# Gated DeltaNet and sparse attention block: decays formed in the place of L, its norms on VectorE, inverse blocks in one transfer each

## What is computed

```
gc = jnp.cumsum(gch, axis=-1)
decay = jnp.exp(jnp.where(incl, gc[..., :, None] - gc[..., None, :], -jnp.inf))
lower = jnp.where(strict, jnp.einsum('bhncd,bhnjd->bhncj', kb, kc) * decay, 0.0)
t_mat = lax.linalg.triangular_solve(lower + eye, jnp.broadcast_to(eye, lower.shape),
                                    left_side=True, lower=True, unit_diagonal=True)
u = jnp.einsum('bhncj,bhnjv->bhncv', t_mat, vb)
w = jnp.einsum('bhncj,bhnjd->bhncd', t_mat, kb * jnp.exp(gc)[..., None])
```

## Time and profile before

| | us |
|---|---|
| median of 3 runs | 929.46 (929.23 to 930.64) |
| the profiled execution, whole time | 928.48 |
| its span (first to last instruction) | 926.7 |
| PE busy in the span | 837.4 |
| DVE, ACT, POOL busy | 461.5, 321.5, 411.3 |
| granted TensorE clock, mean | 0.971 of full |

### The profile page before, as it was taken

The page is one execution under the profiler, slowest core; times in us unless marked ns, Lnnn a source line. Parts: engine busy times, 40 slices in busy tenths (PEclk is TensorE's granted clock), DMA queues, the critical chain, the costliest instruction groups (busy, mean ns, idle before and its releaser), DMA issues.

```text
span 926.7 us, 11375 instructions
## 1 busy us (share of the span) xinstructions
PE 837.4 (90%) x4226; PEld 675.1 (73%) x4226; DVE 461.5 (50%) x859; ACT 321.5 (35%) x654; POOL 411.3 (44%) x302
## 2 busy tenths in 40 slices
PE   1979776893999989999999999999999999999996
PEld 0547554672888867888888877777777778878896
DVE  3356744951676797556666642544435423313104
ACT  2425213331434334344353444424434331221211
POOL 1213586422546534454363553544335434443542
PEclk9989897996999999999999999999999999999998
DMA  7923241034333322333232222222232326453502
GB/s 276 335 81 128 84 115 37 1 91 105 103 92 94 92 69 56 105 87 94 51 100 69 69 69 69 68 69 69 72 87 68 91 90 189 131 162 111 177 29 91
DMA packets 139569, 92.10 MB, mean 99 GB/s; under 512 B 18417, under 2 KB 129266, under 8 KB 138490
## 3 DMA queue, kind: packets, MB, share of 16 engines
q1 hardware_dynamic: 139514, 91.37, 33.7%
HBM read 84.52 MB, written 6.83 MB: 99 GB/s over the span
## 4 chain that ended last, share of the span: by engine, by line
PE 68%; DVE 15%; POOL 5%; ACT 4%; issue 3%; DMA 3%; SPq 2%; POOLq 0%; ACTq 0%; DVEq 0%
PE ps L592 15%; PE ps L594 15%; PE ps L593 15%; PE ps L633 3%; PE ps L863 2%; DVE yq L1568 2%; PE ps L911 2%; PE ps L910 2%; PE ps L909 2%; PE ps L850 2%; DVE binv L1617 2%; ACT prob L1145 2%; DVE kraw L1568 1%; DMA w_ada_sb<-in_w_ada 1%; SPq L520 1%
## 5 line engine op out<-in xcount | busy, mean ns | idle before, releaser
L1217 POOL TENSOR_TENSOR w_lo<-raw,w_hi 128x1024 fp32r<-128x1024 f32 (+1 forms) x109 | 262.9, 2418 | 349.8 <-ACT w_hi L930 349.8
L592 PE MATMUL ps<-h_hi,w_hi 128*128 128x512 f32 (+1 forms) x680 | 291.8, 429 | 6.0 <-ACT h_hi L952 6.0
L594 PE MATMUL ps<-h_hi,w_lo 128*128 128x512 f32 (+1 forms) x680 | 269.5, 396 | 0.0
L593 PE MATMUL ps<-h_lo,w_hi 128*128 128x512 f32 (+1 forms) x680 | 268.1, 394 | 0.0
L592 PEld LDWEIGHTS ps<-h_hi,w_hi 128*128 128x128 f32 (+1 forms) x680 | 130.3, 192 | 32.5 <-ACT h_hi L952 6.8
L594 PEld LDWEIGHTS ps<-h_hi,w_lo 128*128 128x128 f32 (+1 forms) x680 | 129.0, 190 | 29.9 <-issue 0.3
L593 PEld LDWEIGHTS ps<-h_lo,w_hi 128*128 128x128 f32 (+1 forms) x680 | 130.2, 191 | 26.3 <-issue 3.7
L930 ACT ACTIVATE w_hi<-raw 128x1024 fp32r<-128x1024 f32 (+1 forms) x109 | 113.4, 1050 | 29.7 <-PE ps L911 17.1
L1086 ACT ACTIVATE o_tok<-ps 128x128 f32<-128x128 f32 x32 | 8.9, 278 | 105.1 <-PE ps L815 104.9
L633 PE MATMUL ps<-w_ada_sb,cb 128*128 128x512 f32 x64 | 29.3, 617 | 11.4 <-DMA w_ada_sb<-in_w_ada 11.4
L910 PE MATMUL ps<-w_lo,y_hi 128*128 128x256 f32 x128 | 36.2, 283 | 0.0
(11 more groups left out here) (276 smaller groups left out, 1478.2 us busy)
## 6 DMA issues: line engine op xcount, KB each, us to landing
raw<-in_w_in SPq DMA_DIRECT2D x84, 512.0 KB, 3.8
w_ada_sb<-in_w_ada SPq DMA_DIRECT2D x8, 1024.0 KB, 19.4
raw<-in_w_b_out SPq DMA_DIRECT2D x8, 512.0 KB, 4.0
raw<-in_w_a_out SPq DMA_DIRECT2D x8, 512.0 KB, 4.5
ada<-in_w_ada SPq DMA_DIRECT2D x8, 512.0 KB, 4.9
raw<-in_w_o SPq DMA_DIRECT2D x8, 512.0 KB, 4.1
x_sb<-in_x SPq DMA_DIRECT2D x1, 2048.0 KB, 9.8
inverse_tiles<-zero SPq DMA_DIRECT2D x8, 256.0 KB, 2.9
```

The costliest lines, as they stand in the source:

```text
L592: pe.matmul(out_ap, w_hi[:, slot, k, 0:m], rhs_hi(k), start=(k == 0), stop=False)
L593: pe.matmul(out_ap, w_hi[:, slot, k, 0:m], rhs_lo(k), start=False, stop=False)
L594: mm = pe.matmul(out_ap, w_lo[:, slot, k, 0:m], rhs_hi(k), start=False, stop=(k == KT - 1))
L1217: pool.tensor_tensor(w_lo[:, slot, :, 0:n], raw[:, slot, :, 0:n], w_hi[:, slot, :, 0:n].bitcast(F32), ALU.subtract).then_inc(lo_made, 1)
```

## The change

1. `Dl` is no longer used for the keys' decays. Right after the decays are in DRAM (round 7), SP loads the rows of all 8 heads directly in the places L[:, h]. POOL adds only the mask (one operation, rounds `R_LOW`), ACT takes the exponential in place, in four operations of 128x128 whose bias is the decay column (so the subtraction on POOL goes).
2. DVE adds epsilon, takes the reciprocal (the square of the norm's inverse), multiplies by -beta, and writes L in four operations of 128x128 that take products, row scale and decay at once. POOL keeps the power -0.5 and two columns, after L is made.
3. `R_GRAM` is 13, 15, 17, 19, 22, 26, 74, 90 in place of 13, 16, 19, 22, 25, 28, 74, 90, and the first batch's inversion begins at round 25 in place of 34; its store nine rounds later. The store of L is issued 2 rounds after a gram, the blocks 4 after (3 and 5 before).
4. The DRAM tiles are padded so that the diagonal blocks of all tiles lie at one stride: blocks are read with one transfer of 32 blocks (512 pieces of 64 B) per head, and the inverses written with two transfers of 128 blocks (2,048 pieces each) in place of 32. Clearing is 2 transfers in place of 8, from a zero tile of 2,064 columns (512 before) in the place where the indexer's queries come later, for which ACT's copy now waits.

```diff
-R_GRAM = [13, 16, 19, 22, 25, 28, 74, 90]
-R_INV = [34, 97]
+R_LOW = [10, 11, 13, 14, 17, 18, 46, 50]
+R_GRAM = [13, 15, 17, 19, 22, 26, 74, 90]
+R_INV = [25, 97]
...
         def key_decay(h):
...
-            sp.dma_start(Dl[:, h % 2].rearrange("p i f -> p (i f)"), gc_dram[h:h + 1, :].to_broadcast([P, S])).then_inc(s_pa[h % 2], 16)
+            sp.dma_start(L[:, h].rearrange("p i f -> p (i f)"), gc_dram[h:h + 1, :].to_broadcast([P, S])).then_inc(s_low[h], 16)
...
+        def sub_blocks(ap, h, count):
+
+            return bass.AP(ap.tensor, ap.offset + h * NT * TILE, [[STEP, count], [P, SUB], [1, SUB]])
...
-            for t, src in enumerate(sub_blocks(l_dram, h)):
-                at = 32 * (h % 4) + 8 * t
-                sp.dma_start(binv[at:at + 8, 0], src).then_inc(s_blk[h // 4], 16)
+            sp.dma_start(binv[32 * (h % 4):32 * (h % 4) + 32, 0], sub_blocks(l_dram, h, 32)).then_inc(s_blk[h // 4], 16)
...
             for n in range(2):
-                for hh in range(4):
-                    for t, dst in enumerate(sub_blocks(inv_dram[n], hh)):
-                        at = 32 * hh + 8 * t
-                        sp.dma_start(dst, binv[at:at + 8, 1 + n]).then_inc(s_inv[b], 16)
+                sp.dma_start(sub_blocks(inv_dram[n], 0, P), binv[:, 1 + n]).then_inc(s_inv[b], 16)
...
         def low_decay(h):
-            act.wait_ge(*low_pool.at("ylo", h))
-            act.activation(Dl[:, h % 2], Dl[:, h % 2], ACT.Exp, scale=-1.0).then_inc(*low_act.inc("d"))
+            act.wait_ge(*low_pool.at("m", h))
+            for i in range(NT):
+                ins = act.activation(L[:, h, i, :], L[:, h, i, :], ACT.Exp, bias=gcol(GC, h, i), scale=-1.0)
+            ins.then_inc(*low_act.inc("d"))
...
-            pool.tensor_tensor(L[:, h], L[:, h], per_tile(kst[:, LCOL, h, :]), ALU.mult).then_inc(*gram_pool.inc("L"))
...
+            dve.tensor_scalar(kst[:, SS, h, :], kst[:, SS, h, :], 4.0 * EPS, None, ALU.add).then_inc(*gram_dve.inc("eps"))
...
+            dve.reciprocal(kst[:, RK2, h, :], kst[:, SS, h, :]).then_inc(*gram_dve.inc("rk2"))
...
+            dve.tensor_tensor(kst[:, LCOL, h, :], kst[:, RK2, h, :], gvec(NBETA, h), ALU.mult).then_inc(*gram_dve.inc("lcol"))
...
-            dve.tensor_tensor(L[:, h], tiles(bank(5)), Dl[:, h % 2], ALU.mult).then_inc(*gram_dve.inc("L"))
+            for i in range(NT):
+                ins = dve.scalar_tensor_tensor(out=L[:, h, i, :], in0=ps[:, 5, blk(i)], scalar=kcol(LCOL, h, i),
+                                               in1=L[:, h, i, :], op0=ALU.mult, op1=ALU.mult)
+            ins.then_inc(*gram_dve.inc("L"))
```

More of the change, by code:

```diff
@@ L223, in program @@
     gcT = place("gcT", [HEADS, S], at=where["P_b"])
-    zero = place("zero", [P, S], at=where["U"] + ROW)
+    zero = place("zero", [P, 4 * NT * (P // SUB) * (SUB * P + SUB) // P], at=where["kd"])
     relu = place("relu", [P, 2, S], at=where["th"] + 4 * ROW)
@@ L263, in program @@
     gc_dram = nc.dram_tensor("gc_rows", (HEADS, S), F32).ap()
-    l_dram = nc.dram_tensor("lower_tiles", (HEADS, P, NT, P), F32).ap()
-    inv_dram = nc.dram_tensor("inverse_tiles", (2, 4, P, NT, P), F32).ap()
+    STEP = SUB * P + SUB
+    TILE = P // SUB * STEP
+    l_dram = nc.dram_tensor("lower_tiles", (HEADS * NT * TILE,), F32).ap()
+    inv_dram = nc.dram_tensor("inverse_tiles", (2, 4 * NT * TILE), F32).ap()
     ps = ctx.enter_context(nc.psum_tensor("ps", [P, 8, S], F32))
@@ L327, in program @@
     s_gct, s_zero = sem("decay_rows_stored"), sem("inverse_tiles_zeroed")
-    s_pa = [sem("key_decay_loaded0"), sem("key_decay_loaded1")]
+    s_low = [sem(f"key_decay_loaded{h}") for h in range(HEADS)]
     s_pb = sem("query_decay_loaded")
@@ L489, in query_decay, with whole_tiles @@
             sp.dma_start(P_b[:], gc_dram[h:h + 1, :].to_broadcast([P, S])).then_inc(s_pb, 16)
+        def whole_tiles(ap, h):
+            return bass.AP(ap.tensor, ap.offset + h * NT * TILE, [[P, P], [TILE, NT], [1, P]])
         def store_lower(h):
[L492 to L498, removed]
+            sp.wait_ge(*gram_dve.at("L", h))
+            sp.dma_start(whole_tiles(l_dram, h), L[:, h]).then_inc(s_lst[h], 16)
+        def sub_blocks(ap, h, count):
+            return bass.AP(ap.tensor, ap.offset + h * NT * TILE, [[STEP, count], [P, SUB], [1, SUB]])
         def lower_blocks(h):
@@ L510, in store_inverse @@
             if b == 0:
[L511 removed]
+                sp.wait_ge(s_zero, 2 * 16)
             else:
@@ L553, in _ @@
                 sp.dma_start(gc_dram[:], gcT[:]).then_inc(s_gct, 16)
+                sp.wait_ge(s_gct, 16)
+                for h in range(HEADS):
+                    key_decay(h)
             for h in range(HEADS):
-                if r == R_GRAM[h] - 4:
-                    key_decay(h)
                 if r == R_DELTA[h] - 5:
                     query_decay(h)
-                if r == R_GRAM[h] + 3:
+                if r == R_GRAM[h] + 2:
                     store_lower(h)
-                if r == R_GRAM[h] + 5:
+                if r == R_GRAM[h] + 4:
                     lower_blocks(h)
```

58 lines of the change are left out of this document (22 added, 36 removed).

## The result

The changed kernel takes **899.3 us** (median of 4, 898.37 to 900.11), the kernel before 930.05 (929.23 to 930.76) beside it: a ratio of 0.967, 95% interval 0.965 to 0.969. The profiled execution took 899.64 us with a span of 897.8, against 928.48 and 926.7, so 28.9 us of span went (between the medians it is 30.8; the profiled execution of before was a short one). The forecast was 893.0 with a range of 884 to 907.

A forecast was written before the change was run, and what follows sets the result against it. PE was taken as the bound, short of work mainly between 93 and 232 us, waiting for L, logits and U. 12.2 + 5 + 17.7 + 1.7 = 36.6 us off 926.7 gave 893 us as the median, range 884 to 907.

The forecast's parts named there:

- C: Wait for U ahead of Z16 of head 0: gone whole, 17.7 us gained, bounds 14 and 17.7.
- D: Z16 to the dU16 matmuls: no lower clock after the long wait, 1.7 us gained, between 1 and 2.
- A: Grams up to the first logit: fewer large POOL operations on L, 12.2 us gained, bounds 5 and 16.
- L0 is then ready at 108.1: Head 0's L, before at 105.68; PE waits from about 100 to 108 us and restarts at the lower clock.
- with little idle between: DVE after L0, through taps, grams 2 to 4 and swish: L4 made at 129.0 us.
- the lower bound: A's low case, 5 us: small DVE operations of three heads each held behind a `w_lo`.
- B: Logits, rounds 28 to 43: 40.8 us instead of 45.7, term of 5 us, bounds 0 and 8.
- DVE comes late to it: Logits: DVE reaches first scores at 140, PE its first logit at 134, costing about 3 us.
- Rival 1: Only the wait for U goes; A and B give 5 us or less: 905 to 909 us, chance 0.16.
- Rival 2: DVE does not hold PE; A at its upper end, B free of waits: 886 us, chance 0.15.
- Rival 3: Transfers of 2,048 pieces cost by the piece, 24.3 us each, making U late: around 945 us, chance 0.05.
- At nothing: Clearing, broadcast loads, ACT's split exponential, SP's order, and heads 1 and 2 (-1 to +2 us): all taken as 0.

The follow-up runs named there:

- run 8: Changed kernel with the first inversion from round 30 instead of 25, all else kept: 898.8 us, ratio 0.967.
- run 4: Changed kernel with the first inversion from round 34 instead of 25, nothing else changed: 904.5 us, ratio 0.972.
- run 3: Changed kernel with grams and inversion in the rounds of before and masks two rounds before each gram: 895.3 us, ratio 0.962.
- run 9: run 3 with norm and row scale of L back on GpSimd, early decays and single transfers kept: 915.3 us, ratio 0.985.
- run 10: Kernel before with GpSimd forming each head's decay three rounds before its gram instead of two: 919.1 us, ratio 0.988.
- run 11: run 9 with the mask additions of heads 1 to 5 one round earlier: 903.5 us, ratio 0.971.
- run 5: run 3 with the first inversion from round 30 instead of 34: 890.9 us, ratio 0.959.
- run 7: run 5 with the mask additions in the places of the changed kernel: 893.7 us, ratio 0.961.
- run 12: run 5 with masks of heads 2, 4 and 5 one to two rounds earlier and inversion from round 31: 888.9 us, ratio 0.956.
- run 1: Kernel before with only blocks of L in one transfer a head and inverses in two, plus padding: 922.7 us, ratio 0.991.

## Why the prediction was right, and where it was wrong

The direction and the range were right, and so was the large term. **C** was 17.7 and is 17.7, **D** 1.7 and 1.65. The reason given for C, that U's load has its place behind others and the writes are long out, holds: SP issued the writes at 168.34 and U's load at 190.03. Both came later than my layout had them (155 and 181). Z16 was late as well (197.45 for 189), by nearly as much as U's load, and so the wait stayed away. The transfers of inverses between 160 and 200 us landed 5.2 to 6.1 us after their issue, so U was there by 196.1. Of the 4 us of slack that I counted 1.3 to 2.2 were there.

**A** was mis-sized: 12.2 for 7.5. "L0 is then ready at 108.1" is exact: 109.38, less the 1.35 of scatter. So is DVE's chain of 3.15 us (106.20 to 109.38; its terms as written add up to 3.07), and the wait of "about 100 to 108". L of head 1 was also where the same steps put it: 113.5 on the prediction's clock, for 108.1 + 2.05 + 3.15 = 113.3. What failed is the sentence after, that DVE then runs through "with little idle between". To the L of head 4 it lists 14.75 us of work and allows 15.7; it took 18.6. In head 2 the small operations fell beside POOL's `w_lo` and a mask, which only the lower bound had priced:

```profile
118.38 1.55 DVE L1587 TENSOR_SCALAR kst<-kst 128x4 f32<-128x4 f32 x1
...
120.18 0.97 DVE L1591 TENSOR_TENSOR kst<-kst,gsc 128x4 f32<-128x4 f32 x1
```

where 0.17 each is their time alone. That is 2.2 us. PE waited 3.50 us ahead of gram 3 for that L, ran at the lower clock behind it (run 8), and so DVE waited in turn: the grams share one bank, DVE can't take the next before PE has made it, and PE can't make it before DVE has read the last. DVE's waits in after between 95 and 140 us are

```profile
DVE diag L1583 <- PE ps L698: 3.5, 3, 1.6
```

of which the first, 1.6, lies in the stretch that came out as forecast, and 0.7 and 1.2 ahead of heads 3 and 4. The second drop of the clock was not in the forecast, which had one restart only. Gram 5 came at 134.2 on the prediction's clock, for 130.6, and the first logit at 138.9 for 134.2; of the 1.1 us added between the two, 0.9 was a wait for iq.

The Trainium skill, "SBUF — State Buffer", section "Who interferes with whom", has the multiplication by -beta held and the four operations that read PSUM not. The trace agrees on the first: L1591 took 0.97. No group of L1595 fell beside a large operation of POOL in after, so their 1.12 or 1.13 us don't test the second; the product of before with the same kind of inputs does, the L at 122.17 us, which took 0.69 though `w_lo` ran from 121.43 to 123.80. The addition of eps has only one input in SBUF and was held too; the section counts its kind as one that can be, by a mode in which it uses both ports.

**B** was 5 for 3.2. "DVE comes late to it" was right and priced too low, at some 3 us. In before the stretch of 60.4 us holds 5.9 of waits and some 2 at the lower clock; without them it is 52.5. In after PE waits 4.7 us in it, 4.3 for relu (3.0 before) and 0.4 for iq, and 52.5 + 4.7 is the 57.2 measured. Runs 4 and 3 show what early inversion costs there, 2.8 us and more.

**The cause given under A was incomplete**, and this is the error behind the rest. It said that every L waits for two decay operations held up by POOL's scaling and power, so by how long POOL's work is. Runs 9 to 11 show that it was above all where the work stands: behind a chain that waits for DVE, with ACT's queue passing the wait on. A single number takes 11.4 us from the kernel before. I had ACT down as an engine with time to spare, which it was, and missed that its order puts the copy of `kraw` behind the exponential. The change breaks the ring three ways at once, by masks early, by `gram` a round later on POOL and by norms off POOL.

**What was not asked at all** is whether the new rounds of the grams are good. The prediction took them as given, though it counted 8 us of waiting for L0 against them. Runs 5, 7 and 8 show that grams two rounds apart lose 5.1 us, and the early masks 2.8 more; with places as in run 12 the same parts give 888.9. That the hand-over of the one bank is what makes close grams dear is read from the waits of PE and DVE on each other; moving the grams also moves DVE's work between them, and no run separates the two.

**Rivals.** Rival 1 (905 to 909) named the right mechanism and overdid it: A and B gave 10.7, not 5 or less. Rival 2 (DVE never holds PE) is what run 5 and run 12 come near, not after. Rival 3: the writes of 2,048 pieces landed after 5 to 6 us in after and at most 8.4 in any run, under the 9 us at which I let it begin to cost. "At nothing" held for clearing and broadcast loads so far as any wait shows it; for everything behind the first solve, heads 1 and 2 among it, the ledger leaves 0.2 us.

The single parts don't add: mask ahead 11.4, single transfers 7.6, both against before, and single transfers zero against after. The wait for U can be removed by issuing faster or by starting earlier, and only once.

## What to carry to other kernels

When an engine waits for a buffer, follow the queues of all engines around the loop and ask what stands behind each waiting instruction; moving a piece of work ahead of the wait (one number here, 11.4 us) can be worth more than making it shorter. Where two engines hand one bank to and fro, try a spacing no closer than the slower side's time per step: here arriving earlier only turned work into idle time and restarts at the lower clock, 5.1 us in run 8 against run 7. And when several parts aim at one wait, test each with the others in place: here a part worth 7.6 us alone was worth nothing beside the others.

## What was unexpected of the hardware

Very small operations on VectorE were held for as long as large ones. In after, a product of the inversion with 4 elements a partition took 2.13 us, its neighbour with 9 took 0.16; POOL's `w_lo` ran from 136.87 for 2.38 us.

```profile
137.15 2.13 DVE L1611 TENSOR_TENSOR binv<-binv 128x4 f32<-128x4 f32 x1
...
143.10 0.16 DVE L1611 TENSOR_TENSOR binv<-binv 128x9 f32<-128x9 f32 x1
```

Two write transfers of 2,048 pieces of 64 B each kept SP's queue 3.45 us in after and 6.33 in run 1, one of them up to 4.7 (run 9), where U's load takes about 0.4; why it differs between runs of nearly the same place stays open. From issue to landing they took 5.2 to 6.1 us in after, and up to 8.4 in run 9.

```profile
168.34 3.45 SPq L515 DMA_DIRECT2D inverse_tiles<-binv  x2
...
190.03 0.42 SPq L521 DMA_DIRECT2D U<-inverse_tiles  x1
```
